# First two up blocks of a float32 decoder layer: where part activations are made, who scales, and when raw places are filled

## The reference, cut to what matters

```python
x = x + merged @ w_out[l]
h = rms_norm(x, g_ffn[l])
u = h @ w_up[l]                    # 2048 x 11264
up = jnp.pad(u, ((0, 0), (CONV_WIDTH - 1, 0), (0, 0)))
conv = sum(wc[t] * up[:, t:t + s] for t in range(CONV_WIDTH)) + b_conv[l]
gate, val = jnp.split(conv, 2, axis=-1)
x = x + (jax.nn.silu(gate) * val) @ w_down[l]
```

## Time and profile before

| what | value |
|---|---|
| median of 3 runs | 1366.07 us (1365.45 to 1368.0) |
| the profiled execution | 1368.29 us, of which the span of the profile is 1366.5 us |
| mean granted TensorE clock | 0.997 |
| TensorE busy | 1352.6 us, 99% of the span |
| VectorE busy | 1083.4 us, 79% |
| ScalarE busy | 829.3 us, 61% |
| DMA | 299.45 MB, 219 GB/s over the span |

### The profile page before, as it was taken

How to read it: one execution, slowest core, us unless ns; L and a number is a source line. 1 busy time by engine, 2 the same in 40 slices (tenths; PEclk the granted TensorE clock), 3 DMA queues, 4 the chain that set the end, 5 groups by cost and what they waited for, 6 DMA issues and landing times.

```text
span 1366.5 us, 16332 instructions
## 1 busy us (share of the span) xinstructions
PE 1352.6 (99%) x6139; PEld 1118.5 (82%) x6139; DVE 1083.4 (79%) x1323; ACT 829.3 (61%) x1033; POOL 129.9 (10%) x149
## 2 busy tenths in 40 slices
PE   8999999999999999999989999999999999999999
PEld 6888888888788888888877888888888888888887
DVE  5646555678878776657688999998989999999985
ACT  6555545466666664446666667676666666666752
POOL 0101010121111000001010201010110102010100
PEclk9999999999999999999999999999999999999999
DMA  9765556577888655567888798888879798888851
GB/s 341 235 201 172 163 183 164 157 219 231 199 227 232 213 169 177 200 230 222 259 236 279 148 308 195 280 227 248 252 203 288 193 284 192 304 177 294 219 182 62
DMA packets 115663, 299.45 MB, mean 219 GB/s; under 512 B 11640, under 2 KB 12928, under 8 KB 115072
## 3 DMA queue, kind: packets, MB, share of 16 engines
q1 hardware_dynamic: 95056, 241.92, 51.7%
q0 software_dynamic: 16448, 52.44, 22.0%
q10 hardware_dynamic: 4080, 4.05, 0.9%
HBM read 296.26 MB, written 2.11 MB: 218 GB/s over the span
## 4 chain that ended last, share of the span: by engine, by line
PE 93%; DVE 3%; ACT 2%; DMA 1%; issue 1%; SPq 0%; ACTq 0%
PE acc L631 16%; PE acc L633 16%; PE acc L632 16%; PE acc L664 7%; PE acc L668 7%; PE acc L666 7%; PE acc L653 3%; PE acc L651 3%; PE acc L649 3%; PE acc L850 2%; PE acc L846 2%; PE acc L848 2%; PE acc L821 2%; PE acc L825 2%; PE acc L823 2%; PE acc L934 1%
## 5 line engine op out<-in xcount | busy, mean ns | idle before, releaser
L1500 DVE TENSOR_TENSOR w_lo<-raw,w_hi 128x1024 fp32r<-128x1024 f32 x259 | 313.3, 1223 | 149.8 <-ACT w_hi L1098 148.2
L1098 ACT ACTIVATE w_hi<-raw 128x1024 fp32r<-128x1024 f32 x259 | 272.4, 1059 | 211.8 <-PE acc L633 179.5
L631 PE MATMUL acc<-w_hi,actA 128*128 128x512 f32 x860 | 341.8, 397 | 2.3 <-DVE w_lo L1500 2.2
L633 PE MATMUL acc<-w_hi,actA 128*128 128x512 f32 x860 | 336.0, 391 | 0.0
L632 PE MATMUL acc<-w_lo,actA 128*128 128x512 f32 x860 | 335.4, 390 | 0.0
L631 PEld LDWEIGHTS acc<-w_hi,actA 128*128 128x128 f32 x860 | 162.0, 188 | 35.4 <-issue 3.3
L633 PEld LDWEIGHTS acc<-w_hi,actA 128*128 128x128 f32 x860 | 161.8, 188 | 34.5
L632 PEld LDWEIGHTS acc<-w_lo,actA 128*128 128x128 f32 x860 | 161.9, 188 | 32.5
L1098 ACT ACTIVATE w_hi<-raw_y 128x1024 fp32r<-128x1024 f32 x120 | 127.1, 1062 | 74.0 <-PE acc L668 18.1
L1500 DVE TENSOR_TENSOR w_lo<-raw_y,w_hi 128x1024 fp32r<-128x1024 f32 x120 | 145.4, 1221 | 20.1 <-ACT w_hi L1098 18.3
L1098 ACT ACTIVATE w_hi<-raw_x 128x1024 fp32r<-128x1024 f32 x90 | 95.4, 1060 | 64.1 <-PE acc L633 30.1
(11 more groups left out here) (246 smaller groups left out, 2254.4 us busy)
## 6 DMA issues: line engine op xcount, KB each, us to landing
raw<-w_in SPq DMA_DIRECT2D x127, 512.0 KB, 4.1
raw_x<-w_up SPq DMA_DIRECT2D x44, 512.0 KB, 6.1
raw<-w_down SPq DMA_DIRECT2D x43, 512.0 KB, 5.5
raw_y<-w_up POOLq DMA_DIRECT2D x35, 512.0 KB, 6.9
raw<-w_up SPq DMA_DIRECT2D x29, 512.0 KB, 6.0
raw<-w_out SPq DMA_DIRECT2D x28, 512.0 KB, 4.3
odd<-w_up SPq DMA_DIRECT2D x27, 512.0 KB, 4.4
odd<-w_up POOLq DMA_DIRECT2D x27, 512.0 KB, 9.0
```

The lines of the kernel that those rows point to most:

```text
L631: nc.tensor.matmul(o, lhsT=a_h, rhs=w_hi[:, s, k, :], start=first and k == 0, stop=False)
L633: mm = nc.tensor.matmul(o, lhsT=a_l, rhs=w_hi[:, s, k, :], start=False, stop=last and k == KU - 1)
L1098: nc.scalar.activation(w_hi[:, n % RING, :, :], src.rearrange("p (k n) -> p k n", k=KU), ACT.Copy).then_inc(hi_done, 1)
L1500: nc.vector.tensor_tensor(w_lo[:, n % RING, :, :], src.rearrange("p (k n) -> p k n", k=KU), w_hi[:, n % RING, :, :].bitcast(f32), ALU.subt ...
```

## The change

It touches the first two up blocks and the raw places.

- The sums and high and low parts of the third pair (`make_more`, `more_high`, `more_low`) are made in block 1 (from P5 and the plain gate units on), in place of block 0. Their sums are put into `odd[1024:2048]`, and not into `work[0:1024]`, so `newest_tap` of block 0 no longer waits for them.
- The scalings of block 0's copies are done by ScalarE with its scale operand (`scaled` in its program, for gate[0], val[0], val[1]), and the copy of gate[1] scales as it copies. The wait for the scale, rs_x, is now in ScalarE's queue.
- A silu of one column is put behind the squares of the last x2 quarter, in front of the first up block.
- The results c11 and c21 of block 0 are made one list position earlier on VectorE, ahead of `low` of ("S", 1, "P6", 0), with a wait for the end of ("U", 0, 0, 3). The last gate tap of block 0 moves behind both sums in place for P7. The turning of block 0's val side moves one unit later.
- SP fills two raw places (5 and 6) at once at position ("U", 0, 1, 1), when plain_low(3) and part P5 are done. Place 7 is only the third raw_y tile, and place 4 is first used for load 27. The loads that followed four plain units of block 0 (`SHIFTED`, now of loads 20 to 23) are held back and issued together at ("S", 1, "P6", 0).

```diff
--- before.py
+++ after.py
@@ -155,19 +155,19 @@
 FIRST_SLOTS = (8, 9, 0, 1, 2, 3)
-MORE_SLOTS = (4, 5, 6, 7)
-ALL_SLOTS = MORE_SLOTS + FIRST_SLOTS
-KEPT_SLOTS = MORE_SLOTS[:2] + FIRST_SLOTS
-NARROW_AT = WIDE_AT + len(ALL_SLOTS)
+MORE_SLOTS = (5, 6)
+NARROW_AT = WIDE_AT + 8
+SLOTS = 10
+SHIFTED = (12, 13, 14, 15)
...
         return FIRST_SLOTS[k % 6]
-    return ALL_SLOTS[k - WIDE_AT] if k < NARROW_AT else KEPT_SLOTS[(k - NARROW_AT) % 8]
+    m = (k - WIDE_AT) % 8
+    return (MORE_SLOTS + FIRST_SLOTS)[m] if k < NARROW_AT or m != 1 else 4
@@ -187,7 +187,7 @@
-X_PLAIN, Y_PLAIN = (WIDE_AT + MORE_SLOTS.index(6), WIDE_AT + MORE_SLOTS.index(7))
+X_PLAIN = WIDE_AT + MORE_SLOTS.index(6)
 PART_AT = {name: n + 1 for n, name in enumerate(STEPS)}
@@ -347,7 +347,7 @@
         def more_sum(m):
-            return work[:, m * KU * P:(m + 1) * KU * P].rearrange("p (k s) -> p k s", k=KU)
+            return odd[:, UNIT + m * KU * P:UNIT + (m + 1) * KU * P].rearrange("p (k s) -> p k s", k=KU)
@@ -377,7 +377,7 @@
             sem("first_tile"), sem("gains_in"), sem("tile_high"), sem("tile_split"), sem("warm_data"))
-        w_loaded = [sem(f"w_loaded{s}") for s in range(len(ALL_SLOTS))]
+        w_loaded = [sem(f"w_loaded{s}") for s in range(SLOTS)]
@@ -578,18 +578,23 @@
                     k = next_in_slot(LOAD_AT[unit])
-                    if k < len(LOADS):
+                    if unit == ("U", 0, 1, 1):
+                        sp.wait_ge(part_lo, PART_AT["P5"])
+                        sp.wait_ge(plain_lo, 2)
+                        for m in range(WIDE_AT, WIDE_AT + len(MORE_SLOTS)):
+                            load_unit(LOADS[m])
+                    if k < len(LOADS) and LOAD_AT[unit] not in SHIFTED:
                         sp.wait_ge(lo_done, n)
...
                 _, i, name, q = unit
-                if unit == ("S", 1, "P1", QU - 1):
+                if unit == ("S", 1, "P6", 0):
                     sp.wait_ge(lo_done, n)
-                    sp.wait_ge(part_lo, len(STEPS))
-                    sp.wait_ge(plain_lo, 2)
+                    for k in SHIFTED:
+                        load_unit(LOADS[next_in_slot(k)])
+                elif unit == ("S", 1, "P2", 0):
                     sp.wait_ge(more_lo, len(STEPS))
-                    for k in range(WIDE_AT, WIDE_AT + len(MORE_SLOTS)):
-                        load_unit(LOADS[k])
+                    load_unit(LOADS[NARROW_AT + 1])
                 if name == "P5":
@@ -606,7 +611,7 @@
                     if i == FULL - 1 and q == QU - 1:
-                        sp.wait_ge(lo_done, AT[LOADS[Y_PLAIN]])
+                        sp.wait_ge(more_lo, len(STEPS))
                         load_b22(FULL, QU)
@@ -1033,7 +1038,7 @@
                     turn_x2(3)
-                if name == "P1" and q == 0 and i:
+                if name == "P1" and q == (1 if i == 1 else 0) and i:
                     turn_val(i - 1)
@@ -1370,8 +1375,6 @@
                 act.wait_ge((gate_ready, val_ready)[side], i + 1)
-                if i == 0 and not side:
-                    act.wait_ge(more_lo, len(STEPS))
                 if side:
@@ -1383,6 +1386,10 @@
+            def scaled(part, r):
+                act.wait_ge(rs_x, 2)
+                nc.scalar.activation(part, part, ACT.Copy, scale=xrs2[:, r:r + 1]).then_inc(up_scaled, 1)
@@ -1425,8 +1432,9 @@
                     act.wait_ge(used, n + 1)
-                    nc.scalar.activation(gate[1], bank[0][:, :], ACT.Copy, scale=xrs2[:, 1:2] if i else 1.0)\
-                        .then_inc(u1_copied, 1)
+                    if i == 0:
+                        act.wait_ge(rs_x, 2)
+                    nc.scalar.activation(gate[1], bank[0][:, :], ACT.Copy, scale=xrs2[:, 1:2]).then_inc(u1_copied, 1)
@@ -1459,17 +1467,26 @@
                         x2_squares(3)
+                        act.wait_ge(warm, 2)
+                        nc.scalar.activation(st[:, 91:92], st[:, 90:91], ACT.Silu)
                     continue
...
                     _, i, side, j = unit
+                    if i == 0 and side == 1 and j == 1:
+                        act.wait_ge(u0_copied, 1)
+                        scaled(gate[0], 0)
+                    elif i == 0 and side == 0 and j == 0:
+                        act.wait_ge(v_copied, 1)
+                        scaled(val[0], 0)
+                        scaled(val[1], 1)
                     if side == 0 and j == 2:
...
                         hidden_high(0)
-                    elif unit == ("U", 0, 1, 2):
+                    elif unit == ("U", 1, 1, 1):
                         for part in ("P3", "P1", "P7", "P6"):
                             more_high(part)
-                    elif unit == ("U", 0, 1, 3):
+                    elif unit == ("U", 1, 1, 2):
                         for part in ("P5", "P2", "P4"):
@@ -1901,13 +1918,6 @@
-            def scaled(i, r, part, order):
-                if i == 0:
-                    if order > 2:
-                        dve.wait_ge(v_copied, 1)
-                    nc.vector.tensor_scalar(part, part, xrs2[:, r:r + 1], None, ALU.mult).then_inc(up_scaled, 1)
-                    dve.wait_ge(up_scaled, order)
@@ -1926,15 +1936,16 @@
                     dve.wait_ge(u0_copied, i + 1)
-                    scaled(i, 0, gate[0], 1)
+                    dve.wait_ge(up_scaled, 1)
                     result(bank[1][:, :], xrs2[:, 0:1], gate[0], c12_done)
...
                         dve.wait_ge(u1_copied, 1)
-                        scaled(0, 1, gate[1], 2)
+                        dve.wait_ge(nrs_ready, 1)
                         result(bank[3][:, :], nrs2[:, 1:2], gate[1], c22_done)
-                elif unit == ("U", i, 0, plain_units(i) - 1):
-                    dve.wait_ge(used, n + 1)
+                elif unit == ("U", 0, 0, 2) or unit == ("U", i, 0, plain_units(i) - 1) and i:
+                    dve.wait_ge(used, AT["U", i, 0, plain_units(i) - 1] + 1)
                     dve.wait_ge(v_copied, i + 1)
+                    dve.wait_ge(up_scaled, 3)
                     result(bank[2][:, :], xrs2[:, 0:1], val[0], c11_done)
@@ -1973,21 +1984,22 @@
                         nc.vector.tensor_scalar(nrs2, xrs2, -1.0, None, ALU.mult).then_inc(nrs_ready, 1)
-                        make_more()
-                    elif side == 1 and j == 3 and i == 0:
+                    elif side == 1 and j == 2 and i == 1:
                         for part in ("P3", "P1", "P7", "P6"):
                             more_low(part)
-                    elif side == 0 and j < 2 and i < FULL:
+                    elif side == 1 and j == 3 and i == 1:
+                        for part in ("P5", "P2", "P4"):
+                            more_low(part)
+                    elif side == 0 and j < 2 and i < FULL and (i or j == 0):
                         older_tap(i, 0, 1 - j)
-                        if i == 0:
-                            scaled(0, j, val[j], 3 + j)
                     continue
...
                     x2_norm()
-                elif i == 0 and name == "P2" and q == 0:
-                    for part in ("P5", "P2", "P4"):
-                        more_low(part)
+                elif i == 1 and name == "P5" and q == 1:
+                    make_more()
+                elif unit == ("S", 1, "P3", 1):
+                    older_tap(0, 0, 0)
                 elif name == "P1" and q == 1 and i:
```

## The result

The changed kernel is slower: 1369.86 us in the median of 13 runs (1368.64 to 1370.93), against 1366.79 for the kernel before (13 runs, 1365.45 to 1368.0). The ratio is 1.0024 with a 95% interval of 1.0016 to 1.0031, so 2.2 to 4.2 us. The forecast was 1365.5 in a range of 1361.5 to 1368.9. Runs in the slow state (one of e6 with 3536.3 us, one of the kernel before, timed beside e9, with 1692.85) are in no median or ratio of this document.

The account below looks back on a forecast made before the run. TensorE, busy 99% of the span, was taken as the bound, with 6.8 us of waits and slow clock to win. P5 earlier (-0.7) and a new wait (+0.3) gave -0.4 from 1366.07: forecast 1365.5, range 1361.5 to 1368.9.

Parts of the forecast that it names:

- the burst: SP silent from 666.4 to 680.2, then nine tiles in a row at 1.26 us each; P3's first lands at 692.2.
- (d): P5 of block 1 waits for the copy of P6's sum, 1.2 before; P5 forecast to start 0.4 to 0.95 earlier.
- VectorE's 11.6 to c21: VectorE in block 0, from w_lo to the end of c21 without a gap: 11.6 us, where it was 13.8.
- 7.1 from the w_hi to L1422: ScalarE's chain from a w_hi to the copy of P6's sum: 7.1 us as before, so the copy at 718.9.
- (a): Second row half of ("U", 0, 1, 0) waits for ScalarE's copy of bank 0; table load and silu add 1.5, idle 1.8.
- (c): Turning of block 0's val side waits for c21; 2.9 before, forecast 2.3.
- ("D", 0, 0): This unit waits 0.2 to 0.3 for block 0's hidden_low, delayed by four sums on VectorE; +0.3 in the sum.
- (b): P4 product of block 0 waits for VectorE's last gate-side result; 0.7 before, forecast to go to nothing.
- ScalarE's wait: ScalarE stands for block 1's P3 tile (raw_y) from 687.6 until 692.4, idle about 5 us.
- The slower rival: SP's nine loads run at a mixed rate; decides from 1.73 us a tile, 1369.7 at 1.85; chance 0.18.
- The first rival: SP's nine loads delay nobody; P5 of block 1 starts at 716.0, -4.6 + 0.3, 1361.8; chance 0.28.
- A second burst: Four plain loads put back to P6 of block 1; ScalarE takes the accumulated x tile at 711.7, not 712.68.

Follow-up runs that it names:

- e6: e5 with block 0's silu one w_hi later in ScalarE's queue; 1363.12 us, ratio 0.9970 to the kernel before.
- e9: e3 with e6's silu edit and the four held loads issued together at ("S", 1, "P1", 0); 1361.56 us, ratio 0.9960 to the kernel before.
- e1: The changed kernel without the one-column silu, so the table load is back in front of block 0's silu; 1367.82 us, ratio 1.0010 to the kernel before.
- e2: The changed kernel with SP's wait and its two fills moved behind the loads of block 1's P3 pair; 1365.89 us, ratio 0.9997 to the kernel before.
- e3: e2 with the one-column silu moved ahead of the last x2 squares, into ScalarE's idle time; 1363.55 us, ratio 0.9982 to the kernel before.
- e4: The kernel before with only the one-column silu behind the squares added; 1368.99 us, ratio 1.0018 to the kernel before.
- e5: e3 with the four held loads each issued again when its own place is free; 1363.87 us, ratio 0.9976 to the kernel before.
- e8: The changed kernel with SP's wait kept but the two fills issued behind P3's pair; 1366.07 us, ratio 0.9999 to the kernel before.
- e10: Second profile of e2, no edits; 71.98 us from the last x2 turning to block 1's gate turning, 69.81 in the first profile.
- e7: Second profile of the changed kernel, no edits; 74.99 us from the last x2 turning to block 1's gate turning, 74.09 in the first profile.

## Why the prediction was wrong

It failed on two terms: the rate at which the burst lands, and the clock behind (d), which was put at nothing.

1. **The rate of the burst.** The prediction took 1.26 us a tile, "since no accumulating tile is under way in that stretch", and P3's first tile 20.2 behind the mark (692.2 on the clock of the profile before). It was in use at 21.4. Of these 1.2, 0.3 is the first landing, 3.5 after its issue where 3.1 was taken. The rest is the rate: the first of the nine landed at 681.7, P3's first at 691.5, 1.39 a tile, and the ninth at 693.1, 1.43 a tile over all. In the burst, windows of 1 us show 344 to 430 GB/s, and the mean of the ten microseconds from 680 is 396, not the 415 of the earlier trace rows. The 1.46 that follows from the limit of about 358 GB/s in the Trainium skill (DMA: Bandwidth & Descriptors, Specifications), which the prediction set aside for the row, gives 21.5 for this tile. Its number was nearer, but not its reason: the 396 is above that limit. The tiles did land in the order of their issue. Everything behind that term held: ScalarE's queue, VectorE's 11.6 to c21, 7.1 from the w_hi to L1422. They carried the 1.2 to 1.5 on to c21 (40.4 for 38.9) and most of it to P5 (48.9 for 47.5 to 48.0; before, 48.5).
2. **The clock behind (d).** The prediction priced a fall of the clock at (a) and at (c), but not at (d). Yet its own sum has (d) at 1.1 to 2.3 (TensorE through at 719.0 or 717.3, P5 at 720.1 or 719.6), and "about 2 or less" among the signs of being right. For the same length at (a) it had said that a fall might come and would cost 1.7. At 1.8 the clock fell, and behind P5 nothing hides it: the nine matmuls from 718.94 took 3.75 us, those from 720.55 before 2.19, 1.6 lost.

P5's lateness 0.4, the clock 1.6, and 0.3 at ("D", 0, 0), as forecast, are the 2.3 by which the stretch is longer; 3.1 in the medians, with 2.2 inside the interval. The forecast had -0.7, 0 and +0.3. It also started from 1366.07, a median of three runs, where thirteen have 1366.79: 0.7 of the distance between 1365.5 and 1369.86 is no fault of the mechanism. That the fall at (a) would be hidden was right in the main only: e1 shows by its stretch that the chain hides 1.8 of the 3.1, and by the medians 2.0 of them are paid.

Right were: (b) gone; the table load's delay of 1.5 at (a), with the next ACTIVATE 0.01 behind the end of the load and without the further 1.38 that the Trainium skill (ScalarE: Activation LUTs, What ACT_TABLE_LOAD costs) gives for a drain; the order in which SP goes silent and then issues nine; ScalarE's wait (4.0 for 5); (c) 2.1 for 2.3; that removing work from both queues would not show. The slower rival was named by its mechanism, the burst at a lower rate, with 1.73 a tile as the point from which it decides; that point was too far off because the fall of the clock behind (d) was not in it.

The first rival, that the burst delays nobody, was put at -4.3. e2 and e3 show how much of it was there: with the burst out of the way 2.0 and 3.3 of stretch, 0.8 and 3.1 in the medians. A second burst, which I had costed as a help ("leave the accumulated x tiles alone on the engines") and not for the P2 pair behind it, took 1.5 to 1.7 of the rest. In the changed kernel the lateness that the first burst had made hid that of the second.

## What to carry to other kernels

A wait in an in-order DMA queue is paid by every load behind it. When a fill has to wait for a place to come free, put it behind the loads that are due next, and ask of each burst which load is issued last in it and who waits for that one: here two fills moved by six positions brought 4.0 us, the table load moved into idle time 2.3, and four loads moved by four positions, with e6's edit, 2.0; together they turned 3 us of loss into 5 of gain. A table load belongs where its engine stands idle; one position further, it cost 2.3 here (e3 against e2, and e4). And a wait on TensorE of the size of (a), (c) and (d) should be priced twice, with and without the fall of the clock, above all the last one, behind which nothing hides it. A term that was priced at one wait is owed the same price at the next of that length.

## What the hardware showed that I had not expected

In this stage the clock fell after 1.8 us of idle time in six of the cases seen ((a) in three profiles; (d) in both of the changed kernel and in e5) and stayed up after 1.8 in four ((a) in three profiles, (d) in e8). After 2.1 it fell once (("D", 0, 0) in e10) and stayed up once ((c) of the changed kernel), and it stayed up even after 2.65 ((c) in e7). So the length of the idle time alone doesn't decide between 1.8 and 2.65; what else decides it, no run here shows. The longer waits of this stage (2.9 in three profiles, 4.0 in e1) came with a fall each time, those of 1.7 and less never. Behind (a) and (d) a fall cost 1.3 to 1.6; at (c) it cost 2.5 in e1 and some 2.8 in e4, where the clock stayed low for longer.

The timed runs have a mean granted clock too, to three digits, and it differs within one kernel. Of the eleven runs of e2 four have 1.000, with a mean time of 1364.9, and seven have less, with 1367.0; of the thirteen of the changed kernel none has 1.000, of the eleven of e3 nine, of the five of e9 all. So how often the clock falls is part of what these changes gain or lose, and it isn't fixed for a kernel. A mean over the run doesn't say where it fell.

A load at the end of a burst is late out of proportion. P2's pair of tiles, with four plain and two accumulated tiles issued in front of it, was in 12.3 to 12.9 us after its issue, as the mean of the two (changed kernel, e2, e3, e8, e10); with the four loads elsewhere it took 6.9 (e5, e9), before the change 5.4, and a single x tile 3.1.
